# A two-layer hybrid decoder trunk: the third mixer's level products, issued block by block

## The reference

```
Bc = jnp.cumsum(gc, axis=1)
diff = jnp.where(causal, Bc[:, :, None] - Bc[:, None, :], 0.0)
wdec = jnp.where(causal, jnp.exp(diff), 0.0)
A = jnp.einsum('bthk,bshk,btshk->bhts', qc, kc, wdec)
o = jnp.einsum('bhts,bshv->bthv', A, vc) + jnp.einsum('bthk,bhkv->bthv', qc * jnp.exp(Bc), S)
```

## Time and profile before

| | us |
|---|---|
| median of 3 runs | 1510.01 (1509.89 to 1512.62) |
| the profiled execution, its own time | 1510.41 |
| its span, first to last instruction | 1508.6 |
| PE busy | 1491.7 (99% of the span) |
| DVE / ACT / POOL busy | 949.4 / 679.6 / 943.7 |

### The profile page before, as it was taken

One profiled execution on the slowest core, in us unless ns is written; L12 is line 12 of the kernel. 1 busy time (PEld: TensorE's weight loads), 2 busy tenths in 40 slices (PEclk: granted clock), 3 DMA queues, 4 the chain that ended last, 5 costly groups with the idle time before them and its releaser, 6 DMA issues.

```text
span 1508.6 us, 26528 instructions
## 1 busy us (share of the span) xinstructions
PE 1491.7 (99%) x10373; PEld 1443.3 (96%) x10373; DVE 949.4 (63%) x1909; ACT 679.6 (45%) x1202; POOL 943.7 (63%) x737
## 2 busy tenths in 40 slices
PE   9999999999999999999999999999999999999997
PEld 8999999999999999999999999999999999999997
DVE  4765357668777777744346643667678777777434
ACT  5834444444444544433357344444443445344332
POOL 7766465555556666787767665555555566767873
PEclk9999999999999999999999999999999999999999
DMA  7533554444545454444434336444454444454442
GB/s 262 174 114 122 158 185 131 140 148 142 180 142 169 127 155 153 144 151 152 141 117 140 123 112 191 152 142 141 137 170 151 128 156 149 145 152 143 153 146 86
DMA packets 66548, 223.37 MB, mean 148 GB/s; under 512 B 8056, under 2 KB 12664, under 8 KB 66424
## 3 DMA queue, kind: packets, MB, share of 16 engines
q1 hardware_dynamic: 66424, 221.67, 46.9%
HBM read 206.07 MB, written 15.58 MB: 147 GB/s over the span
## 4 chain that ended last, share of the span: by engine, by line
PE 93%; DVE 3%; DMA 2%; ACT 2%; issue 1%; POOL 0%; SPq 0%; DVEq 0%; ACTq 0%
PE gps L1424 27%; PE gps L1426 27%; PE gps L1425 27%; DMA raw<-in_w 2%; PE xp L1617 1%; PE xp L1676 1%; PE xp L1674 1%; PE xp L1578 1%; PE xp L1588 1%; PE xp L1667 1%; PE xp L1565 0%; PE xp L1596 0%; PE xp L1572 0%; PE xp L1579 0%; PE gps L1565 0%
## 5 line engine op out<-in xcount | busy, mean ns | idle before, releaser
L659 POOL TENSOR_TENSOR low<-raw,whi 128x512 fp32r<-128x512 f32 x724 | 938.0, 1318 | 542.8 <-ACT whi L680 353.4
L1424 PE MATMUL gps<-xh,whi 128*128 128x320 f32 (+1 forms) x2000 | 637.8, 319 | 2.5 <-DVE xl L914 1.6
L1426 PE MATMUL gps<-xh,low 128*128 128x320 f32 (+1 forms) x2000 | 620.8, 310 | 0.0
L1425 PE MATMUL gps<-xl,whi 128*128 128x320 f32 (+1 forms) x2000 | 620.7, 310 | 0.0
L1424 PEld LDWEIGHTS gps<-xh,whi 128*128 128x128 f32 x2000 | 376.9, 188 | 9.9 <-POOL low L659 1.8
L1425 PEld LDWEIGHTS gps<-xl,whi 128*128 128x128 f32 x2000 | 378.6, 189 | 3.2
L680 ACT ACTIVATE whi<-raw 128x1024 fp32r<-128x1024 f32 x272 | 286.6, 1054 | 208.4 <-PE gps L1426 106.6
L1426 PEld LDWEIGHTS gps<-xh,low 128*128 128x128 f32 x2000 | 378.3, 189 | 0.0
L1424 PE MATMUL gps<-ah,whi 128*128 128x320 f32 x640 | 199.4, 312 | 0.2
L1426 PE MATMUL gps<-ah,low 128*128 128x320 f32 x640 | 198.0, 309 | 0.0
L1425 PE MATMUL gps<-al,whi 128*128 128x320 f32 x640 | 198.0, 309 | 0.0
(11 more groups left out here) (328 smaller groups left out, 1824.8 us busy)
## 6 DMA issues: line engine op xcount, KB each, us to landing
raw<-in_w SPq DMA_DIRECT2D x360, 512.0 KB, 3.5
s<-in_st SPq DMA_DIRECT2D x24, 512.0 KB, 4.2
out_ss<-s SPq DMA_DIRECT2D x24, 512.0 KB, 5.0
con<-in_cst SPq DMA_DIRECT2D x4, 462.0 KB, 4.7
out_sp<-pst SPq DMA_DIRECT2D x24, 64.0 KB, 5.0
mix<-in_x SPq DMA_DIRECT2D x4, 320.0 KB, 5.1
out_y<-mix SPq DMA_DIRECT2D x8, 160.0 KB, 1.9
raw<-in_w SPq DMA_DIRECT2D x4, 256.0 KB, 4.9
```

What stands on the lines that cost most here:

```text
L659: nc.gpsimd.tensor_tensor(low_of(c)[:, half, :], raw[:, c % RAWS, half, :], whi[:, c % HIGHS, half, :].bitcast(F32), ALU.subtract).then_in ...
L1424: M(out, hi, xhi, start=start, stop=False)
L1425: M(out, hi, xlo, start=False, stop=False)
L1426: return M(out, lo, xhi, start=False, stop=stop)
```

## The change

The products of levels 0 to 5 are cut along the stationary columns. Levels 0 to 3 (blocks of at most 32 steps) take 32 stationary columns at a time, and as moving columns only those of the same 32 steps (32 of them in level 0, the 16 late ones in levels 1 to 3). Level 4 (m = 32) takes the two early blocks of 32 of each tile, each against its late block. Level 5 (m = 64) takes the 64 early columns against the 64 late ones. The results lie where they lay, as far as the mask of `take` reads them; the other positions of `xp[0]` to `xp[2]` are no longer written, and DVE zeroes the three banks once at the start. DVE's `take`, its masks and all else stay.

```diff
+            for i in range(3):
+                V.memset(xp[i][:, :], 0.0)
...
                             if h == 0:
-                                last = M(xp[i][0:w_, hd * w_:(hd + 1) * w_], z12[:, 1, hd, lo:lo + w_],
-                                         z12[:, 0, hd, lo:lo + w_], start=hd == 0, stop=hd == H - 1, skip_group_check=True)
+                                for r in range(w_ // 32):
+                                    mine = slice(lo + 32 * r, lo + 32 * (r + 1))
+                                    col = hd * w_ + 32 * r
+                                    last = M(xp[i][32 * r:32 * (r + 1), col:col + 32], z12[:, 1, hd, mine], z12[:, 0, hd, mine],
+                                             start=hd == 0, stop=hd == H - 1, tile_position=(0, 32 * r), skip_group_check=True)
                                 continue
 
                             m = LEVELS[h - 1]
                             z = z12[:, h % 2, hd, lo:lo + w_]
+                            if m == 32:
+                                for r in (0, 2):
+                                    col = hd * w_ // 2 + 16 * r
+                                    last = M(xp[i][32 * r:32 * (r + 1), col:col + 32], z[:, 32 * r:32 * (r + 1)],
+                                             z[:, 32 * (r + 1):32 * (r + 2)], start=hd == 0, stop=hd == H - 1,
+                                             tile_position=(0, 32 * r), skip_group_check=True)
+                                continue
+                            if m == 64:
+                                last = M(xp[i][0:m, hd * m:(hd + 1) * m], z[:, 0:m], z[:, m:2 * m], start=hd == 0,
+                                         stop=hd == H - 1, skip_group_check=True)
+                                continue
+                            if 2 * m <= 32:
+                                for r in range(w_ // 32):
+                                    own_rows = z[:, 32 * r:32 * (r + 1)]
+                                    col = hd * w_ // 2 + 16 * r
+                                    out = xp[i][32 * r:32 * (r + 1), col:col + 16].rearrange("p (b m) -> p b m", m=m)
+                                    last = M(out, own_rows, own_rows.rearrange("p (b two m) -> p b two m", two=2, m=m)[:, :, 1, :],
+                                             start=hd == 0, stop=hd == H - 1, tile_position=(0, 32 * r), skip_group_check=True)
+                                continue
```

## The result

| | before | after |
|---|---|---|
| median of 4 runs, us | 1510.99 (1509.89 to 1512.62) | 1498.86 (1497.87 to 1499.85) |
| span of the profiled execution, us | 1508.6 | 1496.1 |
| DVE busy, us | 949.4 | 953.7 |

The ratio is 0.9918 with a 95% interval of 0.9904 to 0.9932, so 10.3 to 14.5 us less. The forecast was 1499.0.

The account below looks back on a forecast made before the run. PE's own program was taken as the bound. Per layer, passes, issue and shape changes in levels 0 to 5 summed to 6.53 us instead of 12.22; 11.4 us in all off 1510.4 gave 1499.0, range 1496.8 to 1504.5.

Parts of the forecast that it names:

- The price of a pass by its group's load and columns: PE, levels 0 to 5: a pass takes 0.111 us with 128 stationary columns, 59 ns with 64, 32 ns with 32.
- The issue price: PE's bursts of short passes in levels 0 to 3: 11 ns to issue each pass, range 8 to 17 ns.
- the lower end of the range: Whole layer at 8 ns issue per pass: sum 5.93 us, gain 12.6 us, 1497.8; the stated range began at 1496.8.
- A: Rival for the 32-column passes: they start one after the other, 32 ns each; 13.1 us per layer, 1512; chance 0.04.
- B: Rival for the new bursts: issue limits them to 59 ns per pass; 21.7 us per layer, 1529; chance 0.05.
- C: Rival for the 32-column passes: a floor of 25 ns each; gain 2.7 us, 1507.3; chance 0.06 with its neighbourhood.
- Rival D: New passes: loads don't overlap with matmuls sharing their rows, 59 ns per 32-column pass; gain 5.7 us, 1504.7; chance 0.05.
- The change of shape: PE array at each level: 0.32 us there and back, paid anew by levels 2 to 5, 1.28 us per layer.
- The slack: Between DVE's chain behind level 0 and level 1's start: 0.9 us, said to stay as chain and slots move together.
- a new wait before level 1: Sign that the forecast is wrong: PE's list of waits, expected as empty as before, shows one there.
- Rival E: DVE's chain behind level 0 doesn't move forward: PE waits 0.5 us at level 1; 1500, within the forecast's 0.80.
- The memsets: Three on DVE at the start, 0.48 us each: hidden in its 4.16 us wait for constants; otherwise 1.5 us at most.

Follow-up runs that it names:

- levels 0 to 3 alone: Changed kernel with only levels 0 to 3 in blocks of 32 columns, levels 4 and 5 multiplying whole tiles as before; 1501.9 us, ratio to the kernel before 0.9938.
- group by group: Changed kernel with, in levels 0 to 3, all four heads of one 32-column group before the next group; 1504.89 us, ratio to the kernel before 0.9959.
- POOL writing zeros: Changed kernel with POOL writing zeros instead of subtracting for the low parts of slots 21 and 202, left out of the result; one run, 1499.12 us.

## Why the prediction was right, and the step that was not

*The bound.* What PE saved in the levels came back in the time. Levels 12.3 us shorter made a span 12.5 us shorter and a median 12.1 shorter; with levels 0 to 3 alone it was 9.45 in the levels, 9.0 in the span and 9.5 in the median.

*Luck in the last digit.* Forecast and median agree to 0.1 us because two errors cancel. The gain was put at 11.4 us where the levels gave 12.3, and it was taken from 1510.4 where the median of the kernel before, with one run more, is 1510.99.

*The price of a pass by its group's load and columns* held to some hundredths of a microsecond in every form tried: 32 by 16, 32 by 32, 32 by 64, 32 by 128, 64 by 64. Level 4, where only two groups are used and the group sets the pace, was forecast at 0.83 and measured at 0.82; level 5 1.26 and 1.27.

*The issue price was too high.* The sum took 11 ns per pass for levels 0 to 3, as (0.14 us less 51 ns) / 8. Levels 2 and 3 cost 0.87; less the 0.30 for the change of shape that is 0.56 / 64 = 8.8 ns per pass, and the bound set by the groups is 8. The starts in level 2 show that issue is not the limit. Once under way they have gaps of 6 or 7 ns three times and then 12 ns, a round of four every 32 ns. The rest of the 8.8 ns is some 20 ns lost once behind the first round, 33 to 34 ns for four in the second half, and the last passes 17 ns apart. A round of 32 ns is what the prediction gave as the sign, and 32 ns is also the spacing of a group that works alone (the first passes of group by group). Level 0 is 0.8 / 80 = 10 ns, which is the 16 ns of the sample tile's 16 passes and 8.6 for the others. That is nearly the whole difference between 11.4 us forecast and 12.3 seen in the levels, and the lower end of the range (a gain of 12.6) was built on just this. Rivals A, B and C, which put 25 to 59 ns on a pass, fall with it. The Trainium skill's floor of 25 ns between starts ("TensorE: Matmul & The Clock Gate", section "Wait — 56ns, not 53.3ns?") can hold at most for one column group; for the array as a whole the trace disagrees with it, with 8.8 ns per pass over the 64 passes of level 2.

*Rival D* falls with level 4: there it asked for 59 ns from pass to pass in a group and 1.26 us in all, and the level costs 0.82, with a pass of each group every 32 ns. The row of line L1615 over level 0 agrees: matmuls and loads are busy beside each other though all use all 128 rows.

```profile
73.92:75.09 1.17, 0.99 (x80) 0.88 (x80) 1.00 0.11 28
```

The same page of the Trainium skill states that loads overlap with matmuls only in other row groups ("Part 3: Packing small matmuls — row/col tiling"). The traces disagree: in level 4 a load and 32 moving columns together take a group 32 ns.

*The change of shape* was taken as 0.32 and is 0.28 to 0.33; that levels 2 to 5 would pay it anew was right. PEld around level 2 of the changed kernel shows what it is made of, with PE at the same place below:

```profile
89.97 0.19 PEld L1428 LDWEIGHTS gps<-xh,low 128*128 128x128 f32 x1
90.34 0.64 PEld L1637 LDWEIGHTS xp<-mix 128*32 128x32 f32 x64 [0.19 <-issue]
91.01 0.19 PEld L1426 LDWEIGHTS gps<-xh,whi 128*128 128x128 f32 x1
91.12 0.19 PEld L1427 LDWEIGHTS gps<-xl,whi 128*128 128x128 f32 x1
```

```profile
90.11 0.31 PE L1428 MATMUL gps<-xh,low 128*128 128x320 f32 x1
90.34 0.74 PE L1637 MATMUL xp<-mix 128*32 128x16 f32 x64
91.01 0.42 PE L1426 MATMUL gps<-xh,whi 128*128 128x320 f32 x1
91.27 0.31 PE L1427 MATMUL gps<-xl,whi 128*128 128x320 f32 x1
```

Within the dense stream a load begins 0.14 us before its own matmul. At a change of shape, in either direction, load and matmul begin together. That costs 0.09 us before the first narrow pass, 0.10 behind the last one, and 0.11 once more before the second dense matmul, the length by which its load is late: 0.30 in all. In the kernel before, the first load of level 2 (128 columns, the shape of the dense work) ran ahead, at 93.06 for a pass at 93.20, and nothing was lost there.

*The slack was wrong.* The prediction said that chain and slots "both move forward together and the slack stays" at 0.9 us behind level 0. The chain did move forward, by 1.56 us, but it also grew by 0.9, which used the slack up: PE lost 0.06 and 0.08 us there. The prediction had named a new wait before level 1 as a sign of being wrong; it came, but so small that the list of waits does not show it. Rival E had the place and a price of 1 us for a chain that does not move; what happened was a chain that moves further into another engine's work. In the kernel before it already met the same pair of subtractions, late: L1025 took 0.89 us and L1026 1.77. Starting 1.56 us sooner, L1028 meets the first subtraction (1.78) and the short L1027 the second (1.38). The cause is shown from both sides: with level 0 at its old length, and with POOL reading nothing, the 0.9 us and the wait are gone. The table of waits does not show it: DVE's time beside POOL stands in the length of the instruction and not as idle time before it. The durations stood in the trace of before too: the earlier trace rows has the same L1025 of 128 x 512 at 0.89 and at 1.29 us.

*The memsets* were hidden: DVE ran them from 10.13 to 11.70 and still idled 2.41 us before the constants.

```profile
10.13 1.57 DVE L916 MEMSET xp<- 128x512 f32 x3
14.10 1.04 DVE L918 CAST idb<-con 128x128 bf16<-128x128 f32 x1 [2.41 <-DMA prm<-in_par]
```

## What to carry to other kernels

A product whose result is used in blocks should be cut on both sides, stationary and moving, since a pass costs its column group the dearer of the two; and the blocks should be issued so that neighbours in the program use different column groups. Each stretch of narrow products costs some 0.3 us for the change of shape there and back, so a stretch is only worth cutting if it gains clearly more than that. When a stage gets shorter, look at what the engines behind it will now meet: a chain that starts earlier starts beside other work, and its instructions may be longer there.

## What the runs showed of the hardware

- Passes of 32 stationary columns start 6 or 7 ns apart within a round over four column groups, and a round takes 32 ns, so 8 ns per pass. Over whole levels, with their ends, it is 8.8 ns (64 passes) and 10 ns (80, of which 16 use only two groups). The pace is that of the groups, each of which takes 32 ns per pass.
- The first load of a new shape does not run ahead of its matmul, in either direction; there and back this costs 0.28 to 0.33 us.
- With four groups in turn a pass costs 8.8 ns, with eight passes of a group in a row 21 ns. In strict order eight passes at 32 ns each would leave only the last one beside the next group's first, some 29 ns per pass. So PE seems to start passes out of the program's order between groups, but only a few ahead. This is inferred from the starts; the records don't name the pass.
- A float32 matmul and its load cost about the same at equal column counts: 0.111 us for 128 stationary columns, 0.109 per round for 128 moving ones.
- A subtraction of POOL and a DVE instruction with two operands in SBUF exclude each other (0.69 us becomes 1.78, 0.28 becomes 1.38, and the second subtraction takes 1.74 where the first takes 1.30), a POOL memset of the same tile does not. The Trainium skill, "SBUF — State Buffer", section "🔬 SBUF: two separate sides", says just this: the pair of ports is an exclusive lock, and two SBUF inputs contend only with a GpSimd operation that reads SBUF. The traces of the changed kernel and of POOL writing zeros agree with both.
